# Attention of a hybrid diffusion layer: scores and values in three passes of high and low parts

## Chip, core and metric

One core of a Trainium2 chip. The metric is the device time of one execution of the whole layer, in microseconds; three executions of the kernel before took 1878.99 to 1881.01, median 1880.91.

## What is computed

One layer of a diffusion backbone, all in float32: 512 latent tokens and 256 context tokens of width 2048. A gated DeltaNet branch and a softmax attention branch read one joint input projection; both are gated, projected back, merged and projected out. The change touches the attention alone: 8 query heads, 2 key/value heads, head size 128, 512 queries that see 768 keys (256 of the context, 512 latent).

```python
def block_attention(q, k, v):            # Q_BLOCK = 128
    ...
    scale = hd ** -0.5
    def one_block(qi):
        s = jnp.einsum('bqkgd,bskd->bkgqs', qi, k).astype(jnp.float32) * scale
        p = jax.nn.softmax(s, axis=-1).astype(v.dtype)
        return jnp.einsum('bkgqs,bskd->bqkgd', p, v)
    ...
q_lat = axial_rope(head_rms(bq, B_HEADS, q_norm_w), cos, sin)
k_lat = axial_rope(head_rms(bk, B_KV, k_norm_w), cos, sin)
keys = jnp.concatenate([k_ctx, k_lat], axis=1)
vals = jnp.concatenate([v_ctx, v_lat], axis=1)
b_lat = block_attention(q_lat, keys, vals) * jax.nn.silu(bz)
```

## The kernel before, in words

Every engine has its own hand-written program; semaphores order them, and within an engine the order is that of the code. All the large projections are made in three passes: a float32 operand is split into a high part, rounded to the fp32r type by a copy on ACT (`hi_part`, L759, for weights), and a low part, the rest, by a subtraction on VectorE (`lo_part`, L1091). `three` (L1607) multiplies high by high, high by low and low by high into one PSUM bank. The weights come in pieces of 512 KB, read by SyncE into two buffers in turn; a buffer is read again once both parts of its piece are made. Attention alone has plain float32 matmuls, which TensorE does in two recorded passes each.

The attention stretch comes after the projection of the queries (`bq`) and before the merge. In it the projection of the DeltaNet branch (`pa`, 16 pieces) is interleaved with attention: 32 blocks, block i being head h = i // 4 and 128 queries qt = i % 4. Ahead of the blocks the queries of heads 0 to 3 and the keys are transposed (L1874, L1885) into banks 0 to 7, and ACT copies them out (`q_columns`, `khT`).

- **TensorE**, block i: scores of block i + 1 (L1902, L1903; banks 0 and 1 or 2 and 3), at the first block of a head the values of the head before (L1915, bank 6), half a projection piece (bank 7), in the third block of heads 3 to 6 the transposes of the next head's queries (bank 6), and six transposes of block i's probabilities (L1935, banks 4 and 5).
- **ACT**, iteration i: the exponential of block i + 1 (`att_exp`, L1038), in even iterations the high part of the next weights, the copy of the transposed probabilities of block i (L1052, `probsT`), then queries' squares (blocks 0 to 3), a square root (block 4), the queries' copy, and the high part of the gated output (`b_hi`).
- **VectorE**, iteration i: row sum's reciprocal and scaling of block i (L1512), the maximum of block i + 1 (`att_max`, L1489), in each second block of a head `b_parts` (b_tmp, L1497, and b_lo, L1499, which waits for b_hi), then in odd iterations the gating of a finished piece (`pa_gated`, L1506, frees bank 7) and in even ones the low part of the next weights. In iterations 6, 7, 10 and 11 one tile each of heads 4 to 7 is scaled and rotated (`q_tile(1, t)`, L1356 and L1337 to L1342).
- **GpSimd** issues the transfers of the gates and of gated pieces.

After block 31 come the first piece of the merge (`N_MERGE0`), the values of head 7, and the rest of the merge; at the same time the gates and x are read again.

## Time and profile before

| | us |
|---|---|
| median of three executions | 1880.91 |
| the profiled execution | 1878.7 |
| its span, first to last instruction | 1876.5 |
| TensorE busy | 1800.9 (96%) |
| VectorE busy | 909.9 (48%) |
| ScalarE (ACT) busy | 661.4 (35%) |
| GpSimd busy | 278.1 (15%) |

The profile gives each instruction's start and length. A matmul's length covers its way through the array and overlaps the next one's, so the cost of a matmul in a stream is the distance of two starts. The idle time shown before an instruction names what released it. The mean granted clock of TensorE is 0.99 of full speed.

### The profile page before, as it was taken

The page shows a single profiled execution, that of the slowest core. Times are in us where ns is not written, and L with a number is a line of the kernel's source. Part 1 is how long each engine was busy: PE and PEld are TensorE (multiplying, and loading weights), DVE is VectorE, ACT ScalarE, POOL GpSimd, SP SyncE. Part 2 cuts the span into 40 slices and gives each one's busy share as a digit, 9 for nine tenths or more (in the row PEclk, how much of TensorE's full clock was granted, in tenths as well). Part 3 has the DMA queues.
Part 4 walks back from the last instruction along what each step waited for, and adds up shares of the span by engine and source line. Part 5 has one row for each costly group of instructions (what it writes and reads, how often), then busy time and mean ns, then how long its engine had stood idle before and what let it go on. Part 6 is the DMA issues. An engine that isn't in the chain of part 4 may idle for free.

```text
span 1876.5 us, 25273 instructions
## 1 busy us (share of the span) xinstructions
PE 1800.9 (96%) x10174; PEld 1441.6 (77%) x10174; DVE 909.9 (48%) x1595; ACT 661.4 (35%) x1211; POOL 278.1 (15%) x421
## 2 busy tenths in 40 slices
PE   5799999999999999999999999999998889999999
PEld 2367888888787888878888887877875566788887
DVE  1244443556524577545556554754455544453334
ACT  4323332223234555444343435422354333232211
POOL 0000000000003366377000003211000100210000
PEclk9899999999999999999999999999999999999999
DMA  8793112223224666645444337777432222652332
GB/s 303 245 326 124 57 57 57 63 73 90 70 60 153 197 181 182 203 149 146 136 126 131 115 94 226 231 213 211 140 113 87 87 87 73 257 191 96 118 124 101
DMA packets 198685, 267.12 MB, mean 142 GB/s; under 512 B 37073, under 2 KB 135626, under 8 KB 197162
## 3 DMA queue, kind: packets, MB, share of 16 engines
q1 hardware_dynamic: 175241, 192.74, 34.1%
q0 software_dynamic: 15552, 58.62, 9.4%
q10 hardware_dynamic: 7776, 14.16, 2.0%
q8 instruction: 80, 1.31, 0.3%
q14 instruction: 36, 0.29, 0.0%
HBM read 221.96 MB, written 43.52 MB: 141 GB/s over the span
## 4 chain that ended last, share of the span: by engine, by line
PE 85%; ACT 4%; DVE 4%; DMA 4%; issue 2%; POOL 0%; SPq 0%; ACTq 0%; DVEq 0%; POOLq 0%
PE psum L1610 23%; PE psum L1611 22%; PE psum L1612 22%; PE psum L1915 2%; PE psum L1758 2%; PE psum L1707 1%; PE psum L1709 1%; PE psum L1935 1%; PE psum L1902 1%; PE psum L1603 1%; PE psum L1715 1%; DVE w_lo L1091 1%; ACT w_hi L759 1%; PE psum L1711 1%; PE psum L1713 1%
## 5 line engine op out<-in xcount | busy, mean ns | idle before, releaser
L1091 DVE TENSOR_TENSOR w_lo<-w_raw,w_hi 128x1024 fp32r<-128x1024 f32 x232 | 290.7, 1253 | 625.9 <-ACT w_hi L759 625.6
L759 ACT ACTIVATE w_hi<-w_raw 128x1024 fp32r<-128x1024 f32 x232 | 245.6, 1058 | 864.5 <-PE psum L1612 774.6
L1610 PE MATMUL psum<-h_hi,w_hi 128*128 128x512 f32 x1152 | 470.8, 409 | 8.7 <-DVE w_lo L1091 6.4
L1611 PE MATMUL psum<-h_lo,w_hi 128*128 128x512 f32 x1152 | 452.6, 393 | 0.0
L1612 PE MATMUL psum<-h_hi,w_lo 128*128 128x512 f32 x1152 | 452.1, 392 | 0.0
L1610 PEld LDWEIGHTS psum<-h_hi,w_hi 128*128 128x128 f32 x1152 | 218.2, 189 | 68.2 <-issue 19.4
L1612 PEld LDWEIGHTS psum<-h_hi,w_lo 128*128 128x128 f32 x1152 | 217.5, 189 | 48.1
L1611 PEld LDWEIGHTS psum<-h_lo,w_hi 128*128 128x128 f32 x1152 | 218.5, 190 | 36.2
L1161 DVE SCALAR_TENSOR_TENSOR conv_acc<-conv_in,convw,conv_acc 128x772 f32<-128x772 f32 x96 | 98.2, 1023 | 3.4
L1610 PE MATMUL psum<-w_hi,m_hi 128*128 128x512 f32 x256 | 99.6, 389 | 0.0
L1611 PE MATMUL psum<-w_lo,m_hi 128*128 128x512 f32 x256 | 99.6, 389 | 0.0
L1612 PE MATMUL psum<-w_hi,m_lo 128*128 128x512 f32 x256 | 99.6, 389 | 0.0
L593 POOL TENSOR_TENSOR decay_rhs_hi<-consts,g_hi 128x512 fp32r<-128x512 f32 x24 | 27.0, 1126 | 469.4 <-PE psum L1612 407.7
L1610 PE MATMUL psum<-w_hi,h_hi 128*128 128x512 f32 x192 | 75.5, 393 | 2.5 <-ACT gate_stage L1017 1.3
L1612 PE MATMUL psum<-w_hi,h_lo 128*128 128x512 f32 x192 | 74.8, 389 | 0.0
L1611 PE MATMUL psum<-w_lo,h_hi 128*128 128x512 f32 x192 | 74.7, 389 | 0.0
L1611 PE MATMUL psum<-hc_lo,w_hi 128*128 128x256 f32 x256 | 72.3, 283 | 0.0
L1612 PE MATMUL psum<-hc_hi,w_lo 128*128 128x256 f32 x256 | 72.3, 282 | 0.0
L1610 PE MATMUL psum<-hc_hi,w_hi 128*128 128x256 f32 x256 | 71.9, 281 | 0.0
L1610 PE MATMUL psum<-a_hi,w_hi 128*128 128x512 f32 x128 | 57.2, 447 | 10.2 <-DVE pa_stage L1506 10.2
L1758 PE MATMUL psum<-w_raw_mod,silu_c 128*2 128x512 f32 x256 | 52.1, 668 | 7.0 <-DMA w_raw_mod<-w_mod_dram 6.1
L624 POOL TENSOR_TENSOR inv_blocks<-inv_blocks,inv_outer 128x30 f32<-128x30 f32 (+14 forms) x90 | 55.2, 613 | 7.1
(306 smaller groups left out, 2750.3 us busy)
## 6 DMA issues: line engine op xcount, KB each, us to landing
w_raw<-w_in_dram SPq DMA_DIRECT2D x168, 512.0 KB, 3.9
w_raw_mod<-w_mod_dram SPq DMA_DIRECT2D x64, 512.0 KB, 5.7
w_raw_modg<-w_mod_dram POOLq DMA_DIRECT2D x32, 512.0 KB, 4.5
w_raw<-w_out_dram SPq DMA_DIRECT2D x32, 512.0 KB, 3.6
gate_scratch<-gate_stage ACTq DMA_DIRECT2D x48, 256.0 KB, 4.4
w_raw<-w_proj_a_dram SPq DMA_DIRECT2D x16, 512.0 KB, 4.1
w_raw<-w_proj_b_dram SPq DMA_DIRECT2D x16, 512.0 KB, 3.4
gates<-gate_scratch POOLq DMA_DIRECT2D x32, 256.0 KB, 4.0
```

The costliest lines, as they stand in the source:

```text
L593: ins = pool.tensor_tensor(part_t[d][:], mask, g_t[:, col:col + 4].bitcast(f32).unsqueeze(2).to_broadcast([P, 4, P]), ALU.mult)
L624: pool.tensor_tensor(below, below, outer, ALU.add).then_inc(S("block_steps"), 1)
L759: act.activation(part(whi[i % 2], p), part(place, p), ACT.Copy).then_inc(S("w_hi"), 1)
L1091: dve.tensor_tensor(part(wlo[i % 2], p), part(raw_of(n)[0], p), part(whi[i % 2], p).bitcast(f32), ALU.subtract).then_inc(S("w_lo"), 1)
L1161: ins = dve.scalar_tensor_tensor(out=a[:], in0=r[:, tap:tap + 772], scalar=w, in1=a[:], op0=ALU.mult, op1=ALU.add)
L1603: ins = pe.matmul(bank(7, 1, off + t * 8 + it["head"]), a[:, a0:a0 + P], ones[:, 0:1], start=True, stop=True)
L1610: pe.matmul(out_ap, lh, rh, start=first, stop=False, skip_group_check=shared)
L1611: pe.matmul(out_ap, lh, rl, start=False, stop=False, skip_group_check=shared)
L1612: return pe.matmul(out_ap, ll, rh, start=False, stop=last, skip_group_check=shared)
L1707: ins = pe.matmul(ps[:, u, :], kT_of(h, tile), SS[:, d, h, :], start=True, stop=True)
L1758: ins = pe.matmul(bank(b0)[c0:c0 + 2], sc2[:, k, :], part3(place, p)[:, kk, :], start=k < 4, stop=k >= KT - 4)
L1915: ins = pe.matmul(bank(6), kvr[:, t, 256 + kv * P:256 + (kv + 1) * P], PTt[:, t, :], start=(t == 0), stop=(t == NT - 1))
```

## The change

Queries, keys, values and transposed probabilities are each split into a high fp32r part, which ACT's copy out of PSUM now writes, and a low part, which VectorE subtracts; scores and values then go through `three`. The places of the new tiles are buffers that are idle at the time. The copies on ACT that were plain before are now high parts (same instructions); the values get a copy of their own. VectorE gets the subtractions of queries, keys, values and, once a block, probabilities (`pt_lo_part`), and whoever waited for the copy now waits for the low part.

Besides, the order changes. ACT makes the weights' high part and copies the queries ahead of the exponential. TensorE transposes the queries right after the scores, ahead of the projection, and makes the values after the projection half instead of before it. VectorE's `b_parts` is divided: b_tmp stays, b_lo follows the gating of the piece or the weights' low part. The rotation of heads 4 to 7 runs in eight halves, in iterations 5 to 12. Four semaphores for zeroed buffers become one that counts them in the same order.

```diff
     pa_gate = [at(f"pa_gates{i}", [P, 512], A_H + 53248 + 2048 * i) for i in range(2)]
     pa_out = [at(f"pa_stage{i}", [P, 512], A_H + 57344 + 2048 * i) for i in range(2)]
     sqj = at("square_out", [P, P], A_T + 12288)
-    qhT = at("att_qT", [P, HEADS, SEQ], A_H)
-    khT = at("att_kT", [P, KV, TOK], A_H + 16384)
-    PTt = at("probsT", [P, NT, SEQ], A_H + 34816)
+    q_hi = at("att_q_hi", [P, HEADS, SEQ], A_H, f32r)
+    q_lo = at("att_q_lo", [P, HEADS, SEQ], G_V + 16384, f32r)
+    k_hi = at("att_k_hi", [P, KV, TOK], A_H + 16384, f32r)
+    k_lo = [at(f"att_k_lo{kv}", [P, TOK], (A_H + 30720, A_T + 8192)[kv], f32r) for kv in range(KV)]
+    v_hl = at("att_v", [P, NT, 512], A_C + 16384, f32r)
+    pt_hi = at("probsT_hi", [P, NT, SEQ], A_H + 34816, f32r)
+    pt_lo_a = at("probsT_lo_a", [P, 4, 1024], A_C, f32r)
+    pt_lo_b = at("probsT_lo_b", [P, 2, SEQ], G_V + 12288, f32r)
+    pt_lo_c = at("probsT_lo_c", [P, NT, SEQ], A_H, f32r)
     atmp = [at(f"a_tmp{i}", [P, 512], A_C + 2048 * i) for i in range(2)]
     probs = [at(f"probs{i}", [P, TOK], A_H + 47104 + 3072 * i) for i in range(2)]
     cs = at("cos_sin", [P, LT, 128], G_V)
...
             if g["kind"] == "pa":
                 if g["m"] == 0:
                     eng.wait_ge(S("a_lo"), HEADS)
-                    eng.wait_ge(S("kt_evac"), KV)
+                    eng.wait_ge(S("att_lo"), 6)
                 else:
                     eng.wait_ge(S("pa_mul"), g["m"])
             if g["kind"] == "merge":
...
 
             def q_columns(h, b):
                 act.wait_ge(S("qt_ready"), h + 1)
-                act.activation(qhT[:, h, :], bank(b), ACT.Copy).then_inc(S("qt_evac"), 1)
+                act.activation(q_hi[:, h, :], bank(b), ACT.Copy).then_inc(S("qt_evac"), 1)
 
             for kv in range(KV):
                 q_columns(2 * kv, 2 * kv)
                 q_columns(2 * kv + 1, 2 * kv + 1)
                 act.wait_ge(S("kt_ready"), kv + 1)
-                act.activation(khT[:, kv, :], PS[:, (4 + 2 * kv) * 512:(4 + 2 * kv) * 512 + TOK], ACT.Copy).then_inc(
+                act.activation(k_hi[:, kv, :], PS[:, (4 + 2 * kv) * 512:(4 + 2 * kv) * 512 + TOK], ACT.Copy).then_inc(
                     S("kt_evac"), 1)
 
             def att_exp(i):
...
 
             att_exp(0)
             for i in range(32):
+                h, qt = divmod(i, 4)
+                if i % 2 == 0:
+                    hi_part(N_PA0 + i // 2 + 1)
+                if qt == 2 and 3 <= h < 7:
+                    q_columns(h + 1, 6)
                 if i < 31:
                     att_exp(i + 1)
-                if i % 2 == 0:
-                    hi_part(N_PA0 + i // 2 + 1)
-                h, qt = divmod(i, 4)
                 if qt == 0 and h >= 1:
                     act.wait_ge(S("pv_done"), h)
                 act.wait_ge(S("pt_ready"), i + 1)
-                act.activation(PTt[:, :, qt * P:(qt + 1) * P],
+                act.activation(pt_hi[:, :, qt * P:(qt + 1) * P],
                                PS[:, 2048:2048 + TOK].rearrange("p (t n) -> p t n", t=NT), ACT.Copy).then_inc(
                     S("pt_evac"), 1)
                 if i < 4:
                     q_squares(1, i)
                 if i == 4:
                     qk_std(3, 16, 32)
-                if qt == 2 and 3 <= h < 7:
-                    q_columns(h + 1, 6)
+                if i == 1:
+                    act.activation(v_hl[:, :, 0:256], kvr[:, :, 256:512], ACT.Copy).then_inc(S("kt_evac"), 1)
                 if qt == 1 and h >= 1:
                     act.wait_ge(S("b_tmp"), h)
                     act.activation(b_hi[:, h - 1, :], btmp[:], ACT.Copy).then_inc(S("b_hi"), 1)
...
                             ln(dve.tensor_tensor(tab[:, :, 128 * hf + 64 * sn:128 * hf + 64 * sn + 64],
                                                  cs[:, :, 64 * sn:64 * sn + 64], wv, ALU.mult))
 
-            def rope(rows_t, tab_t, nh):
+            def rope_products(rows_t, tab_t, nh):
 
                 x1, x2 = rows_t[:, :, 0:64], rows_t[:, :, 64:128]
                 tv = lambda k: tab_t[:, 64 * k:64 * k + 64].unsqueeze(1).to_broadcast([P, nh, 64])
                 ln(dve.tensor_tensor(rt[0][:, 0:nh, :], x1, tv(0), ALU.mult))
                 ln(dve.tensor_tensor(rt[1][:, 0:nh, :], x2, tv(3), ALU.mult))
+
+            def rope_sums(rows_t, tab_t, nh):
+
+                x1, x2 = rows_t[:, :, 0:64], rows_t[:, :, 64:128]
+                tv = lambda k: tab_t[:, 64 * k:64 * k + 64].unsqueeze(1).to_broadcast([P, nh, 64])
                 ln(dve.tensor_tensor(rt[2][:, 0:nh, :], x1, tv(1), ALU.mult))
                 ln(dve.tensor_tensor(rt[3][:, 0:nh, :], x2, tv(2), ALU.mult))
                 ln(dve.tensor_tensor(x1, rt[0][:, 0:nh, :], rt[1][:, 0:nh, :], ALU.subtract))
                 return dve.tensor_tensor(x2, rt[2][:, 0:nh, :], rt[3][:, 0:nh, :], ALU.add)
 
+            def rope(rows_t, tab_t, nh):
+                rope_products(rows_t, tab_t, nh)
+                return rope_sums(rows_t, tab_t, nh)
+
             def qk_var(count, a0, a1):
                 dve.wait_ge(S("qk_ssq"), count)
                 dve.tensor_scalar(ssq_a[:, a0:a1], ssq_a[:, a0:a1], 1.0 / P, EPS, ALU.mult, ALU.add).then_inc(
...
                 dve.wait_ge(S("qk_std"), step)
                 ln(dve.reciprocal(ssq_a[:, a0:a1], ssq_a[:, a0:a1]))
 
-            def q_tile(j, t):
+            def q_tile(j, t, parts=(0, 1)):
                 rv = bqr[:, t, 512 * j:512 * j + 512].rearrange("p (h n) -> p h n", h=4)
-                sv = ssq_a[:, 16 * j + 4 * t:16 * j + 4 * t + 4].unsqueeze(2).to_broadcast([P, 4, P])
-                ln(dve.tensor_tensor(rv, rv, sv, ALU.mult))
-                rope(rv, qtab[:, t, :], 4).then_inc(S("q_rot"), 1)
+                if 0 in parts:
+                    sv = ssq_a[:, 16 * j + 4 * t:16 * j + 4 * t + 4].unsqueeze(2).to_broadcast([P, 4, P])
+                    ln(dve.tensor_tensor(rv, rv, sv, ALU.mult))
+                    rope_products(rv, qtab[:, t, :], 4)
+                if 1 not in parts:
+                    return
+                rope_sums(rv, qtab[:, t, :], 4).then_inc(S("q_rot"), 1)
 
                 dve.wait_ge(S("q_rot"), 4 * j + t + 1)
 
...
                 dve.tensor_scalar(nmax[:, i:i + 1], nmax[:, i:i + 1], -float(HD ** -0.5), None, ALU.mult).then_inc(
                     S("negmax"), 1)
 
-            def b_parts(h):
+            def b_gated(h):
                 dve.wait_ge(S("pv_done"), h + 1)
                 k = HEADS + h
                 dve.wait_ge(S(f"z_in{k % 2}"), 16 * (k // 2 + 1))
                 dve.tensor_tensor(btmp[:], bank(6), zst[k % 2][:], ALU.mult).then_inc(S("b_tmp"), 1)
+
+            def b_lo_part(h):
                 dve.wait_ge(S("b_hi"), h + 1)
                 dve.tensor_tensor(b_lo[:, h, :], btmp[:], b_hi[:, h, :].bitcast(f32), ALU.subtract).then_inc(S("b_lo"), 1)
 
...
                     dve.wait_ge(S(f"pa_spill{m % 2}"), 16 * (m // 2))
                 dve.tensor_tensor(pa_out[m % 2][:], bank(7), pa_gate[m % 2][:], ALU.mult).then_inc(S("pa_mul"), 1)
 
+            def q_lo_part(h, b):
+                dve.wait_ge(S("qt_evac"), h + 1)
+                dve.tensor_tensor(q_lo[:, h, :], bank(b), q_hi[:, h, :].bitcast(f32), ALU.subtract).then_inc(S("att_lo"), 1)
+
+            def pt_lo_part(i):
+                h, qt = divmod(i, 4)
+                own = slice(qt * P, qt * P + P)
+                dve.wait_ge(S("pt_evac"), i + 1)
+                src = PS[:, 2048:2048 + TOK].rearrange("p (t n) -> p t n", t=NT)
+                if h >= 6:
+                    dve.tensor_tensor(pt_lo_c[:, :, own], src, pt_hi[:, :, own].bitcast(f32), ALU.subtract).then_inc(S("pt_lo"), 1)
+                    return
+                dve.tensor_tensor(pt_lo_a[:, :, own], src[:, 0:4], pt_hi[:, 0:4, own].bitcast(f32), ALU.subtract)
+                dve.tensor_tensor(pt_lo_b[:, :, own], src[:, 4:6], pt_hi[:, 4:6, own].bitcast(f32), ALU.subtract).then_inc(
+                    S("pt_lo"), 1)
+
+            for kv in range(KV):
+                q_lo_part(2 * kv, 2 * kv)
+                q_lo_part(2 * kv + 1, 2 * kv + 1)
+                if kv:
+                    for i in range(2):
+                        dve.wait_ge(S(f"gate_spill{i}"), 16 * len(GATES))
+                dve.wait_ge(S("kt_evac"), kv + 1)
+                dve.tensor_tensor(k_lo[kv][:], PS[:, (4 + 2 * kv) * 512:(4 + 2 * kv) * 512 + TOK],
+                                  k_hi[:, kv, :].bitcast(f32), ALU.subtract).then_inc(S("att_lo"), 1)
+
             att_max(0)
             for i in range(32):
                 dve.wait_ge(S("exp_done"), i + 1)
                 ln(dve.reciprocal(rsum[:, i:i + 1], rsum[:, i:i + 1]))
                 dve.tensor_scalar(probs[i % 2][:], probs[i % 2][:], rsum[:, i:i + 1], None, ALU.mult).then_inc(
                     S("p_norm"), 1)
+                if i:
+                    pt_lo_part(i - 1)
                 if i < 31:
                     att_max(i + 1)
+                if i % 4 == 2 and 3 <= i // 4 < 7:
+                    q_lo_part(i // 4 + 1, 6)
                 if i % 4 == 1 and i >= 5:
-                    b_parts(i // 4 - 1)
+                    b_gated(i // 4 - 1)
                 if i % 2:
                     pa_gated(i // 2)
                 else:
                     lo_part(N_PA0 + i // 2 + 1)
-
+                if i % 4 == 1 and i >= 5:
+                    b_lo_part(i // 4 - 1)
+
+                if i == 2:
+                    dve.wait_ge(S("kt_evac"), 3)
+                    dve.tensor_tensor(v_hl[:, :, 256:512], kvr[:, :, 256:512], v_hl[:, :, 0:256].bitcast(f32),
+                                      ALU.subtract).then_inc(S("att_lo"), 1)
                 if i == 4:
                     qk_var(44, 16, 32)
                 if i == 5:
                     qk_rstd(3, 16, 32)
-                if i in (6, 7, 10, 11):
-                    q_tile(1, (6, 7, 10, 11).index(i))
+                if 5 <= i < 13:
+                    q_tile(1, (i - 5) // 2, ((i - 5) % 2,))
+            pt_lo_part(31)
             lo_part(N_MERGE0 + 1)
-            b_parts(HEADS - 1)
+            b_gated(HEADS - 1)
+            b_lo_part(HEADS - 1)
             for n in range(N_MERGE0, NP):
                 if n > N_MERGE0:
                     lo_part(n + 1)
...
                 h, qt = divmod(i, 4)
                 if i < 2:
 
-                    pe.wait_ge(S("qt_evac"), 2 * i + 2)
-                    pe.wait_ge(S("kt_evac"), i + 1)
+                    pe.wait_ge(S("att_lo"), 3 + 2 * i)
                 else:
                     pe.wait_ge(S("exp_done"), i - 1)
                 if h >= 4 and qt == 0:
-                    pe.wait_ge(S("qt_evac"), h + 1)
+                    pe.wait_ge(S("att_lo"), h + 4)
                 b = 2 * (i % 2)
-                q = qhT[:, h, qt * P:(qt + 1) * P]
+                q = tuple(part[:, h, qt * P:(qt + 1) * P] for part in (q_hi, q_lo))
                 kv = h // (HEADS // KV)
-                pe.matmul(bank(b), q, khT[:, kv, 0:512], start=True, stop=True)
-                pe.matmul(bank(b + 1, 256), q, khT[:, kv, 512:TOK], start=True, stop=True).then_inc(S("sc_ready"), 1)
+                three(bank(b), q, (k_hi[:, kv, 0:512], k_lo[kv][:, 0:512]), True, True)
+                three(bank(b + 1, 256), q, (k_hi[:, kv, 512:TOK], k_lo[kv][:, 512:TOK]), True, True).then_inc(S("sc_ready"), 1)
 
             def values(h):
 
-                pe.wait_ge(S("pt_evac"), 4 * h + 4)
+                pe.wait_ge(S("pt_lo"), 4 * h + 4)
                 if h >= 1:
                     pe.wait_ge(S("b_tmp"), h)
+                if h == 0:
+                    pe.wait_ge(S("att_lo"), 7)
                 if 3 <= h < 7:
 
-                    pe.wait_ge(S("qt_evac"), h + 2)
+                    pe.wait_ge(S("att_lo"), h + 5)
                 kv = h // (HEADS // KV)
                 for t in range(NT):
-                    ins = pe.matmul(bank(6), kvr[:, t, 256 + kv * P:256 + (kv + 1) * P], PTt[:, t, :],
-                                    start=(t == 0), stop=(t == NT - 1))
+                    lo = pt_lo_c[:, t, :] if h >= 6 else pt_lo_a[:, t, 0:SEQ] if t < 4 else pt_lo_b[:, t - 4, :]
+                    v = tuple(v_hl[:, t, half + kv * P:half + (kv + 1) * P] for half in (0, 256))
+                    ins = three(bank(6), v, (pt_hi[:, t, :], lo), t == 0, t == NT - 1)
                 ins.then_inc(S("pv_done"), 1)
 
             scores(0)
...
                 if i < 31:
                     scores(i + 1)
                 h, qt = divmod(i, 4)
+                if qt == 2 and 3 <= h < 7:
+
+                    pe.wait_ge(S("b_tmp"), h)
+                    q_transposes(h + 1, 6)
+                piece(N_PA0 + i // 2, (i % 2,))
                 if qt == 0 and h >= 1:
                     values(h - 1)
-                piece(N_PA0 + i // 2, (i % 2,))
-                if qt == 2 and 3 <= h < 7:
-
-                    pe.wait_ge(S("b_tmp"), h)
-                    q_transposes(h + 1, 6)
                 pe.wait_ge(S("p_norm"), i + 1)
                 if i:
-                    pe.wait_ge(S("pt_evac"), i)
+                    pe.wait_ge(S("pt_lo"), i)
                 for t in range(NT):
                     ins = pe.transpose(PS[:, 2048 + t * P:2048 + (t + 1) * P], probs[i % 2][:, t * P:(t + 1) * P], ident)
                 ins.then_inc(S("pt_ready"), 1)
...
                 if n > N_MERGE0:
                     piece(n)
                 if n == N_MERGE0 + 1:
-                    pe.wait_ge(S("pt_evac"), 32)
+                    pe.wait_ge(S("pt_lo"), 32)
                     pe.wait_ge(S("b_tmp"), HEADS)
                     pe.wait_ge(S("pa_mul"), 16)
                     pe.wait_ge(S("gsum_in"), 16)
```

## Rows read from the trace of the kernel before

**Rows 1.** The page's first part: busy us, share of the span, instructions.

```profile
PE 1800.9 (96%) x10174; PEld 1441.6 (77%) x10174; DVE 909.9 (48%) x1595; ACT 661.4 (35%) x1211; POOL 278.1 (15%) x421
```

**Rows 2.** Stretches: window, length, busy per engine (instructions), TensorE's clock, DMA share, GB/s.

```profile
1387.70:1601.20 213.50, 192.70 (x805) 132.76 (x805) 108.74 (x204) 88.75 (x161) 19.18 (x35) 1.00 0.28 86
...
1613.00:1629.00 16.00, 16.00 (x65) 11.87 (x64) 7.02 (x9) 4.54 (x6) 2.15 (x4) 1.00 1.01 395
```

**Rows 3.** Timeline of TensorE, block 9: start, us, instruction [idle before].

```profile
1446.20 0.82 PE L1935 MATMUL psum<-consts,probs 128*128 128x128 f32 x6
1446.85 1.02 PE L1902 MATMUL psum<-att_kT,att_qT 128*128 128x512 f32 x2
...
1448.38 0.40 PE L1611 MATMUL psum<-a_lo,w_hi 128*128 128x512 f32 x1
...
1450.92 0.82 PE L1935 MATMUL psum<-consts,probs 128*128 128x128 f32 x6
```

**Rows 4.** The same in the convolution stage: six passes of 256 columns lie between.

```profile
301.60 0.28 PE L1610 MATMUL psum<-hc_hi,w_hi 128*128 128x256 f32 x1
...
302.31 0.40 PE L1610 MATMUL psum<-h_hi,w_hi 128*128 128x512 f32 x1
```

**Rows 5.** The same, one head's values and the projection pass behind.

```profile
1438.18 5.42 PE L1915 MATMUL psum<-probsT,kv_rows 128*128 128x512 f32 x12 [0.61 <-ACT probsT L1052]
...
1443.66 0.39 PE L1611 MATMUL psum<-a_lo,w_hi 128*128 128x512 f32 x1
```

**Rows 6.** Transposes of probabilities: all (ns, first and last start), then blocks 4, 12, 28.

```profile
L1935 PE MATMUL psum<-consts,probs x192: 270/272/331, 1393.6 to 1601.1; 128*128 128x128 f32 x192
...
1417.61 0.82 PE L1935 MATMUL psum<-consts,probs 128*128 128x128 f32 x6
...
1474.52 0.82 PE L1935 MATMUL psum<-consts,probs 128*128 128x128 f32 x6
...
1586.02 0.82 PE L1935 MATMUL psum<-consts,probs 128*128 128x128 f32 x6
```

**Rows 7.** Timeline of three engines, blocks 13 to 15, the gaps of a head.

```profile
1481.45 0.69 DVE L1499 TENSOR_TENSOR b_lo<-b_tmp,b_hi 128x512 fp32r<-128x512 f32 x1 [3.02 <-ACT b_hi L1063]
1482.06 0.68 DVE L1506 TENSOR_TENSOR pa_stage<-psum,pa_gates 128x512 f32<-128x512 f32 x1
...
1482.80 0.50 PE L1610 MATMUL psum<-a_hi,w_hi 128*128 128x512 f32 x1 [1.45 <-DVE pa_stage L1506]
...
1488.41 1.10 PE L1902 MATMUL psum<-att_kT,att_qT 128*128 128x512 f32 x2 [1.48 <-ACT att_qT L1025]
```

**Rows 8.** Groups, 1380 to 1600: busy us, mean ns | idle before, releasers.

```profile
L1489 DVE TENSOR_REDUCE neg_max<-psum 128x1 f32<-128x768 f32 x32 | 30.6, 955 | 44.8 <-PE psum L1903 44.8
L1038 ACT ACTIVATE probs<-psum,neg_max 128x768 f32<-128x768 f32 x32 | 28.9, 902 | 73.8 <-DVE neg_max L1490 72.1 <-ACT square_out L888 1.5
...
L1052 ACT ACTIVATE probsT<-psum 128x768 f32<-128x768 f32 x31 | 25.1, 810 | 48.2 <-PE psum L1935 48.1
L1611 PEld LDWEIGHTS psum<-a_lo,w_hi 128*128 128x128 f32 x128 | 24.1, 188 | 6.4 <-issue 1.7
...
L1091 DVE TENSOR_TENSOR w_lo<-w_raw,w_hi 128x1024 fp32r<-128x1024 f32 x17 | 20.8, 1226 | 33.3 <-ACT w_hi L759 33.3
L1512 DVE TENSOR_SCALAR probs<-probs,row_sum 128x768 f32<-128x768 f32 x32 | 19.9, 621 | 1.1
...
L888 ACT ACTIVATE square_out<-bq_rows 128x128 f32<-128x128 f32 x16 | 5.0, 309 | 0.4
...
L1337 DVE TENSOR_TENSOR rope<-bq_rows,q_tab 128x256 f32<-128x256 f32 x4 | 1.7, 425 | 0.1
```

**Rows 9.** Timeline of the start: first copies, first scores, first projection pass.

```profile
1385.81 1.12 ACT L1025 ACTIVATE att_qT<-psum 128x512 f32<-128x512 f32 x2
...
1387.78 1.10 PE L1902 MATMUL psum<-att_kT,att_qT 128*128 128x512 f32 x2 [0.87 <-ACT att_kT L1031]
...
1390.64 0.59 PE L1610 MATMUL psum<-a_hi,w_hi 128*128 128x512 f32 x1
```

24 lines of the change are left out of this document (12 added, 12 removed).

## Prediction

> **What bounds the kernel now.** I read the page's busy times first: TensorE is busy 96% of the span [rows 1]. So only two things shorten this kernel: fewer TensorE cycles, or fewer of the few gaps it has. Next the busy times by stretch: the attention stretch, from the first scores to the last transposes, takes 213.5 us with TensorE busy 192.7, at a granted clock of 1.00 [rows 2]; some 21 of the kernel's 76 idle microseconds lie there, more than anywhere behind the opening. Then the timeline of one block of 128 queries, which gives the real cadence of the matmuls (the mean duration of one overlaps its neighbour's and is too long): transposes 1446.20 to 1446.85, so 0.65 us; then the scores and twelve passes of the projection, until the next transposes at 1450.92 [rows 3]. Eleven of these passes lie between 1448.38 and 1450.92: 0.231 us each for 512 columns. Twelve take 2.77, so of the block's 4.72 us the scores have 4.72 - 0.65 - 2.77 = 1.30 us.
>
> **TensorE's own work.** Passes of fp32r tiles with 256 columns come six in 302.31 - 301.60, 0.12 us each [rows 4]. New scores: 3 x 0.231 + 3 x 0.12 = 1.05, saving 0.25 in each of 32 blocks: 8.0 us. Values before: from 1438.18 to the second projection pass at 1443.66, less that one pass, 5.25 us a head [rows 5]. New: 18 passes x 0.231 = 4.16, saving 1.09 in each of 8 heads: 8.7 us. Together 16.7 us, all on TensorE, which is the bound. A plain block becomes 1.05 + 2.77 + 0.65 = 4.47 us, one with values 8.63, one with the four query transposes (heads 4 to 7) 4.47 + 4 x 0.11 = 4.91.
>
> **The gaps it has.** The transposes of blocks 12 and 28 begin at 1474.52 and 1586.02 [rows 6], so a later head takes 27.9 us. In each of these heads TensorE waits 1.45 us for pa_stage, since VectorE had stood 3.02 us before b_lo for ACT's b_hi, with pa_stage queued behind it; and 1.48 us for att_qT, the queries' copy queued behind w_hi and probsT on ACT [rows 7]. The four blocks and one set of values cost 4 x 4.72 + 5.25 = 24.1 us, 24.6 with query transposes; so 3.3 us a head are gaps. From the first transposes (1393.6) to those of block 31 (the last of six starts at 1601.1 [rows 6], the first 0.55 earlier) are 207.0 us; its work is 31 x 4.72 + 7 x 5.25 + 4 x 0.44 - 1.3 (no scores in the last) = 183.5; gaps 23.5 in all.
>
> **What VectorE gets.** A subtraction reading PSUM, 512 wide, takes 0.68 and releases VectorE after 0.61; 1024 from SBUF 1.23 [rows 7, 8]; the nearest row for 256 is a rope product, 0.43, and the next instruction follows 0.36 later. pt_lo (512 + 256) is then 0.97 us; q_lo 0.61; k_lo 0.88; v_lo (1536) by the line through 512 and 1024 1.77, and its ACT copy 1.5. No row shows such a subtraction with this strided output. Bounds for pt_lo: 0.88 (one pass of 768 with its overlap taken off; a reduction of 768 takes 0.96 [rows 8]) to 1.4 (two full ones of 512); I take 0.97, nearest in size and source. All together VectorE gains 32 x 0.97 + 8 x 0.61 + 2 x 0.88 + 1.77, some 40 us of work. New waits: transposes of block i wait for pt_lo of i-1, which itself waits for pt_hi (0.81); scores wait for q_lo and k_lo; values wait for pt_lo and v_lo.
>
> **A steady head, walked through.** Times from the start t of the transposes of a values block (block 4h). Durations are those of rows 8, with about 0.05 us from one engine to the next, as in rows 7. pt_hi starts at t + 0.87, pt_lo runs 1.72 to 2.69, though the next scores are ready at 1.90. The reduction and scaling hold VectorE 1.10 (to 3.79), exp runs 3.87 to 4.90 with its accumulator read. b_gated goes in the gap, to 4.40; pa_gated waits for the projection, 4.67 to 5.28: bank 7 is wanted at t + 4.47 + 0.65 + 1.05 = 6.17, so the 1.45 us stall goes. b_hi now stands behind pt_hi and ends at 6.66, b_lo at 7.31; only VectorE waits. Then normalising (0.73) to 8.04 and pt_lo to 9.0, 9.13 for TensorE, which comes to the second transposes after t + 4.47 at 8.94 (9.38 with query transposes): a stall of 0.19 or none. The w_lo of this block starts at once, since ACT made w_hi before the exponential, and q_lo goes in the same way. The third block ends 0.5 before TensorE needs it, and in the fourth the values' 4.16 us let VectorE catch up. The queries' copy, now before the projection, is 2.8 us of work ahead of the next need: that 1.48 goes too. A head takes 3 x 4.47 + 8.63 + 0.44, or + 0.19, 22.5 us instead of 27.9. From block 12 to 28: 90.0 instead of 111.5, gain 21.5. Blocks 28 to 31: 14.5 become 3 x 4.47 + 0.19 - 1.05 = 12.55, gain 1.9.
>
> **Heads with rotation (blocks 5 to 12).** The halves put a scaling and two products (1.64) or two products and two sums (1.84) [rows 8] into every block instead of 3.5 in every other. Per four blocks VectorE has 4 x 2.8 for normalising, pt_lo and reduction, 2 x 1.15 for w_lo, 4 x 0.61, and 7.0 of rotation: 22.9, plus some 2 of waits on ACT. That is above TensorE's 22.0: here VectorE paces. Walked block by block the transposes of blocks 6, 7, 8, 10 and 11 come late by 2.1, 1.3, 0.6, 1.9 and 1.3 us. Blocks 4 to 12 then take 51.8 instead of 56.9 (1417.61 to 1474.52 [rows 6]). Gain 5.1.
>
> **The first four blocks.** The values' copy (1.5) follows ACT's four squares of block 1 (0.31 each and a read of the accumulator behind it [rows 8]); behind it wait w_hi and the third exp; VectorE then does w_lo and v_lo (1.77). The transposes of block 3 come 2.1 us late, and block 4 is reached after 24.1 us, as before. Gain 0, where the passes alone would give 2.1.
>
> **The start.** Scores 0 began at 1387.78, after two queries' copies and a key's [rows 9]. VectorE's three subtractions each follow theirs and end 0.9 later; six in all hold VectorE until 1390.65 (first copy done 1386.43, the copies' pace until 1387.7, then three of 0.61 to 0.88). The first projection pass wants k_lo 1 and scores 1: 1391.0 instead of 1390.64; transposes 0 start 0.2 later. Loss 0.2.
>
> **The end.** The last values save 1.1, but a DMA-full stretch follows, share 1.01 from 1613 [rows 2], in which the weights of the next merge piece are awaited. Between nothing and 1.1: I take 0.5. The renamed zeroing semaphore counts the same memsets in the same order: nothing. No DMA is added, and the reloads come as their buffers come free, 9 us a piece against some 4 to land.
>
> **Sum.** -0.2 + 0 + 5.1 + 21.5 + 1.9 + 0.5 = 28.8. The profiled execution took 1878.7 (span 1876.5 and 2.2 around it), the median is 1880.9; I take the gain from each: 1849.9 for a profiled run, **1852** for the median. Of the 28.8, some 16 are cheaper passes and 13 gaps closed.
>
> **Where a page differs.** Loads and passes overlap in these rows: a load is 188 ns [rows 8], longer than the 0.12 between 256-column passes. The Trainium skill (TensorE: Matmul & The Clock Gate, Part 3, The mechanism) says that weight loads overlap running matmuls only with different row groups; here all rows are used by every pass. By that rule added loads would stand on the path; the trace disagrees. The same page allows, in its Part 2, a background buffer, which agrees.
>
> **Rivals.** (a) The passes get cheaper and the gaps stay: VectorE's new work fills what the reordering freed, so that each head keeps its 3.3 us. Gain 16.7 less the 0.6 at the end and 0.2 at the start: 1865. For it: VectorE holds the transposes now. Against: the walk leaves slack in three blocks of four. 15%. (b) The gaps go almost fully, since halves of the rotation slip into slack I counted as used: 23 + 16 = 39, 1842. 5%. (c) Weight loads don't hide for the added passes: 336 loads (6 x 32 + 18 x 8) instead of 224, 112 x 0.19 = 21 us: 1873. Against it the rows above. 2%. (d) Slower: VectorE becomes the bound everywhere, because a subtraction from PSUM with this output pattern is far dearer. A steady head's VectorE work is 16.6 and its waits 1.4; it ties with the old 27.9 when pt_lo costs 3.4 us, and at 4.4 each head takes 31.7, or 30 us more than before: 1911. 3%, as no shape in the trace is above 1.3 ns a column. (e) The new tiles aren't taken as fp32r, and three full passes run: 2 x (32 x 1.30 + 8 x 5.25) = 167 us more, 2048. The tiles are declared as those of the projection, 1%.
>
> **From these to the numbers.** The forecast has 74%, with its own range 1845 to 1860 (pt_lo between 0.88 and 1.4 moves the rotation blocks and a little of each head: -1 to +8; the end and the start by 1). Taking in most of (a) gives 1845 to 1865. What counts as no change here is within 0.2%, 3.8 us, about what a measurement can tell. Faster 0.95, same 0.01, slower 0.04.
>
> **What would show it.** In the changed profile: six score passes in 1.05 us and eighteen of values in 4.16; plain blocks every 4.47 us; the stalls on pa_stage and att_qT gone; transposes waiting for pt_lo only in the rotation blocks; heads after block 12 every 22.5 us. Heads of 25 us or more, with transposes waiting for pt_lo throughout, would make (a) right and this wrong; a b_lo or w_lo on the critical chain would show that the walk's order on VectorE is off.

## The result, and the profile after

| | before | after |
|---|---|---|
| median of four executions, us | 1879.95 | 1854.88 |
| lowest to highest | 1876.03 to 1881.01 | 1851.49 to 1855.64 |
| the profiled execution | 1878.7 | 1851.49 |
| its span | 1876.5 | 1849.2 |

After to before is 0.9868, with a 95% interval of 0.9856 to 0.988: the change takes 25.1 us off, where 28.8 were forecast. The page of after answers to [rows 1]:

```profile
PE 1781.2 (96%) x10286; PEld 1456.5 (79%) x10286; DVE 947.0 (51%) x1662; ACT 661.9 (36%) x1212; POOL 277.5 (15%) x421
```

TensorE has 112 matmuls more and 19.7 us less to do; VectorE has 37.1 us more. The stretch of [rows 2], 213.50 us long before, is now the first line below. The second line runs from the first transposes of probabilities to those of block 31, and is the yardstick for all that follows (window, length, then busy us and instructions of TensorE, its weight loads, VectorE, ACT and GpSimd, granted clock, DMA share, GB/s):

```profile
1386.30:1573.50 187.20, 175.60 (x904) 145.24 (x905) 142.40 (x268) 88.78 (x162) 19.08 (x35) 1.00 0.32 98
1391.95:1573.50 181.55, 170.51 (x881) 141.06 (x881) 137.88 (x260) 84.36 (x155) 19.08 (x35) 1.00 0.32 96
```

The same yardstick in the kernel before:

```profile
1393.60:1600.60 207.00, 186.43 (x780) 128.41 (x778) 105.42 (x197) 84.81 (x155) 19.18 (x35) 1.00 0.27 83
```

I call the start of block i's six transposes T(i) and the start of the first query transposes Q. What lies ahead of Q is not touched by the change, and Q itself came anywhere from 1379.5 to 1386.0 in the profiled runs below; so kernels are compared by stretches between these starts, and whole times only by their medians. A block is named by the transposes that end it: block i lasts from T(i - 1) to T(i). TensorE's timeline of after, which answers to [rows 6], shows where transposes still wait. The lines are T(0), T(3), T(4), T(6), T(12) and T(31):

```profile
1391.95 0.82 PE L1998 MATMUL psum<-consts,probs 128*128 128x128 f32 x6
...
1407.28 0.85 PE L1998 MATMUL psum<-consts,probs 128*128 128x128 f32 x6 [1.79 <-DVE probsT_lo_b L1544]
1415.84 0.81 PE L1998 MATMUL psum<-consts,probs 128*128 128x128 f32 x6
...
1427.08 0.84 PE L1998 MATMUL psum<-consts,probs 128*128 128x128 f32 x6 [2.15 <-DVE probsT_lo_b L1544]
...
1467.55 0.82 PE L1998 MATMUL psum<-consts,probs 128*128 128x128 f32 x6
...
1573.50 0.85 PE L1998 MATMUL psum<-consts,probs 128*128 128x128 f32 x6 [0.22 <-DVE probsT_lo_c L1541]
```

| us | before | after | gain | forecast |
|---|---|---|---|---|
| ahead of Q | 1383.69 | 1381.87 | 1.8 | none of the change's |
| Q to T(0) | 9.91 | 10.08 | -0.2 | -0.2 |
| T(0) to T(4) | 24.01 | 23.89 | 0.1 | 0 |
| T(4) to T(12) | 56.91 | 51.71 | 5.2 | 5.1 |
| T(12) to T(28) | 111.50 | 93.02 | 18.5 | 21.5 |
| T(28) to T(31) | 14.58 | 12.93 | 1.65 | 1.9 |
| behind T(31) | 275.90 | 275.70 | 0.2 | 0.5 |
| T(0) to T(31) | 207.00 | 181.55 | 25.5 | 28.5 |

In the profiled pair 1.8 us of the 27.2 between the two executions lie ahead of Q and are none of the change's. The row that came out differently is the steady heads, those behind block 12. A head of them has blocks of 4.48, 4.90, 5.36 and 8.56 us from one T to the next; the forecast had 4.47, 4.91, 4.47 and 8.63. The third is block 15 and its like, whose scores are the first of the next head. All three engines there, after:

```profile
1475.06 0.59 ACT L1031 ACTIVATE att_q_hi<-psum 128x512 fp32r<-128x512 f32 x1
...
1476.51 0.95 DVE L1510 TENSOR_REDUCE neg_max<-psum 128x1 f32<-128x768 f32 x1
...
1476.93 0.82 PE L1998 MATMUL psum<-consts,probs 128*128 128x128 f32 x6
...
1477.57 0.68 DVE L1533 TENSOR_TENSOR att_q_lo<-psum,att_q_hi 128x512 fp32r<-128x512 f32 x1
...
1478.39 0.47 PE L1671 MATMUL psum<-att_k_hi,att_q_hi 128*128 128x512 f32 x1 [0.65 <-DVE att_q_lo L1533]
...
1479.16 0.28 PE L1671 MATMUL psum<-att_k_hi,att_q_hi 128*128 128x256 f32 x1
...
1486.77 0.39 PE L1671 MATMUL psum<-probsT_hi,att_v 128*128 128x512 f32 x1
...
1490.85 0.82 PE L1998 MATMUL psum<-consts,probs 128*128 128x128 f32 x6
```

The queries' high part is made by 1475.65, but the low part stands on VectorE behind the maximum of block 15, which holds it to 1477.57, and the scores of block 16, ready to start at 1477.5 when the transposes end, wait for it. The two lines at the end, start of the values and start of the next transposes, give the 18 passes of the values 4.08 us. And the groups of after that answer to [rows 8] (busy us, mean ns of one | idle before, releaser):

```profile
L1543 DVE TENSOR_TENSOR probsT_lo_a<-psum,probsT_hi 128x512 fp32r<-128x512 f32 x24 | 16.5, 686 | 14.8 <-ACT probsT_hi L1060 14.8
L1544 DVE TENSOR_TENSOR probsT_lo_b<-psum,probsT_hi 128x256 fp32r<-128x256 f32 x24 | 10.0, 415 | 0.0
L1541 DVE TENSOR_TENSOR probsT_lo_c<-psum,probsT_hi 128x768 fp32r<-128x768 f32 x8 | 7.6, 955 | 10.6 <-ACT probsT_hi L1060 10.6
L1580 DVE TENSOR_TENSOR att_v<-kv_rows,att_v 128x1536 fp32r<-128x1536 f32 x1 | 1.8, 1752 | 0.0
```

The waits of the attention stretch, after (who waits for whom: us in total, times, longest):

```profile
DVE b_lo L1522 <- ACT b_hi L1071: 9.4, 7, 1.4
PE psum L1998 <- DVE probsT_lo_b L1544: 7.7, 5, 2.2
PE psum L1671 <- DVE att_q_lo L1533: 2.5, 4, 0.6
```

Two of the three gaps of [rows 7] are gone: no matmul waits for pa_stage, none for the queries' copy. The third, b_lo behind b_hi, is there still, 1.4 us at most instead of 3.02. In the steady heads TensorE waits for nothing that is queued behind it. In block 6 it does: behind this b_lo VectorE has the first rotation and pt_lo, for which T(6) waits 2.15 us.

```profile
1422.65 0.69 DVE L1522 TENSOR_TENSOR b_lo<-b_tmp,b_hi 128x512 fp32r<-128x512 f32 x1 [1.44 <-ACT b_hi L1071]
```

### The profile page after: what moved, and what is told of

It reads as the page before. It is cut to its first block, busy times and chain, and to the rows that moved or that the text cites. A ratio compares the mean times of both kernels' runs of the same rounds, so it can differ in the third digit from the quotient of the medians.

```text
span 1849.2 us, 25568 instructions
## 1 busy us (share of the span) xinstructions
PE 1781.2 (96%) x10286; PEld 1456.5 (79%) x10286; DVE 947.0 (51%) x1662; ACT 661.9 (36%) x1212; POOL 277.5 (15%) x421
## 4 chain that ended last, share of the span: by engine, by line
PE 82%; DVE 7%; DMA 4%; ACT 4%; issue 2%; POOL 1%; SPq 0%; ACTq 0%; DVEq 0%; POOLq 0%
PE psum L1671 23%; PE psum L1673 22%; PE psum L1672 22%; PE psum L1819 2%; DMA w_raw_mod<-w_mod_dram 1%; PE psum L1768 1%; PE psum L1770 1%; DVE w_lo L1099 1%; PE psum L1664 1%; PE psum L1776 1%; ACT w_hi L765 1%; PE psum L1772 1%; PE psum L1774 1%; DMA w_raw<-w_proj_b_dram 1%; PE psum L1998 1%
## 5 line engine op out<-in xcount | busy, mean ns | idle before, releaser
L1672 PEld LDWEIGHTS psum<-w_lo,m_hi 128*128 128x128 f32 x256 | 48.0, 188 | 10.1
L1673 PEld LDWEIGHTS psum<-w_hi,m_lo 128*128 128x128 f32 x256 | 48.0, 188 | 10.0
```

The lines of the kernel that those rows point to most:

```text
L1672: pe.matmul(out_ap, lh, rl, start=False, stop=False, skip_group_check=shared)
L1673: return pe.matmul(out_ap, ll, rh, start=False, stop=last, skip_group_check=shared)
```

## The experiments

Two theories stood at the start. **O**: the order alone closes the gaps, and most of the gain is the order's. **P**: cheaper passes are what pays, and the order only makes room for VectorE's new work. The prediction booked both, 16 us to the passes and 13 to the gaps. After that came the stall on q_lo, and what VectorE's work costs. e6, e7, e9 and e10 were executed once each, so their stretches are read and not their whole times. Stretches of all kernels, in us:

| kernel | Q to T(0) | T(0) to T(4) | T(4) to T(12) | T(12) to T(28) | T(28) to T(31) | T(0) to T(31) |
|---|---|---|---|---|---|---|
| before | 9.91 | 24.01 | 56.91 | 111.50 | 14.58 | 207.00 |
| after | 10.08 | 23.89 | 51.71 | 93.02 | 12.93 | 181.55 |
| e1 order only | 9.90 | 24.03 | 49.72 | 97.89 | 12.83 | 184.47 |
| e2 passes only | 10.08 | 30.70 | 71.17 | 116.21 | 15.60 | 233.68 |
| e3 q_lo first | 11.66 | 23.48 | 51.65 | 89.50 | 12.92 | 177.55 |
| e4 values' parts later | 10.12 | 21.97 | 51.69 | 93.01 | 12.93 | 179.60 |
| e5 scores only | 10.08 | 23.01 | 48.95 | 93.84 | 12.35 | 178.15 |
| e6 ACT's old order | 11.65 | 25.29 | 57.94 | 113.15 | 15.00 | 211.38 |
| e7 pt_lo twice | 10.07 | 26.54 | 58.87 | 101.72 | 15.25 | 202.38 |
| e8 all moved | 11.68 | 21.91 | 44.87 | 89.49 | 12.92 | 169.19 |
| e9 TensorE's old order | 10.09 | 27.72 | 58.72 | 98.42 | 12.93 | 197.79 |
| e10 VectorE's old order | 10.10 | 23.88 | 59.77 | 95.72 | 14.35 | 193.72 |

### The order alone: e1_order_only

The kernel before, with float32 matmuls and no low parts, in the order of after:

```
+                if qt == 2 and 3 <= h < 7:
+                    q_columns(h + 1, 6)
                 if i < 31:
                     att_exp(i + 1)
...
-                if qt == 0 and h >= 1:
-                    values(h - 1)
                 piece(N_PA0 + i // 2, (i % 2,))
+                if qt == 0 and h >= 1:
+                    values(h - 1)
```

with the weights' high part likewise ahead of `att_exp`, `b_parts` divided, and the rotation in halves, as in after.

> The kernel before with the changed order alone (w_hi and queries' copy ahead of the exponential, query transposes ahead of the projection, values behind it, b_lo behind the gating, rotation in halves), float32 matmuls kept. Theory O (the order closes the gaps, whatever the matmuls cost): TensorE's work from the first to the last transposes stays 183.5 us and of the 23.5 us of gaps at most 3 stay, so 184 to 187 us instead of 207.0, in all some 1859 (1857 to 1861), ratio 0.988 to 0.990. Rival A (passes and order add up as the result's 25 us less 16.7 for cheaper passes): 8 to 9 us from the order, 1871.

Median 1851.95 against 1875.22, ratio 0.9873 (0.9859 to 0.9888). The stretch took 184.47 us. Its work, by the prediction's cadences, is 183.5; of 23.5 us of gaps 1.0 is left. Its window:

```profile
1391.80:1576.00 184.20, 182.99 (x778) 128.54 (x777) 104.95 (x197) 83.76 (x154) 18.84 (x35) 1.00 0.31 95
```

Theory O holds: the order alone gives 22.5 of the 25.5 us that the stretch gained, without one cheaper pass, and the two medians' ratios are not told apart.

### The passes alone: e2_passes_only

After's parts and passes, with all four orders (ACT's, TensorE's, the two of VectorE's) put back:

```
-                piece(N_PA0 + i // 2, (i % 2,))
                 if qt == 0 and h >= 1:
                     values(h - 1)
+                piece(N_PA0 + i // 2, (i % 2,))
...
-                if 5 <= i < 13:
-                    q_tile(1, (i - 5) // 2, ((i - 5) % 2,))
+                if i in (6, 7, 10, 11):
+                    q_tile(1, (6, 7, 10, 11).index(i))
```

> The changed kernel with its subtractions and three passes but the order of before. Theory O: the work falls by 16.7 us, yet pt_lo and q_lo lengthen the two chains on which a head waited (pa_stage behind b_hi, scores behind the queries' copy), so that each head still takes 26.5 to 28 us and the whole 1870 to 1880. Rival A (they add up): 1863 to 1865, heads of 25.8 us (27.9 less 4 x 0.25 and 1.09).

Median 1900.73 against 1875.22, ratio 1.0142 (1.0115 to 1.0168): 25 us slower than before, and worse than either theory had it. The window and the waits:

```profile
1390.30:1624.00 233.70, 186.24 (x881) 151.69 (x881) 138.34 (x260) 85.31 (x156) 19.28 (x35) 0.93 0.24 74
```

```profile
PE psum L1670 <- DVE probsT_lo_b L1544: 12.7, 6, 4.8
PE psum L1670 <- DVE pa_stage L1529: 12.0, 7, 1.8
PE psum L1997 <- DVE probsT_lo_b L1544: 10.7, 4, 3.7
PE psum L1670 <- DVE att_q_lo L1533: 10.2, 4, 2.6
```

The low parts of the probabilities and of the queries are now waits of TensorE: the values (L1670 behind probsT_lo_b) wait for the last block's, the transposes for the same, the scores for q_lo, which waits for ACT's copy behind the exponential. The old wait for pa_stage is there too. Cheaper passes in the old order cost more than they bring. That also explains why the two parts do not add: with the order, the passes give 184.47 - 181.55 = 2.9 us; without it they cost 233.68 - 207.00 = 26.7. The clock has a share in it, some 10 us (mean of the stretch 0.93; see the last section).

### The three orders one by one: e6_act_order, e9_pe_order, e10_vector_order

Each is after with one engine's order put back. e6: ACT makes the exponential first, then the weights' high part, the probabilities' copy, and the queries' copy behind these.

```
-                if qt == 2 and 3 <= h < 7:
-                    q_columns(h + 1, 6)
                 if i < 31:
                     att_exp(i + 1)
...
+                if qt == 2 and 3 <= h < 7:
+                    q_columns(h + 1, 6)
```

> The changed kernel with ACT's old order: w_hi behind the exponential, the queries' copy behind the probabilities' copy. Theory: the three orders (ACT, TensorE, VectorE) carry the passes together; this one alone undone makes w_lo wait for w_hi in every second block and the next head's scores for q_hi: heads of 26 us, stretch 200 to 208. Rival (only the VectorE order counts): within 2 us of 181.6.

1888.23 us, stretch 211.38, 29.8 more than after. ACT, VectorE and TensorE in it, at the scores of a new head:

```profile
1492.27 0.80 ACT L1058 ACTIVATE probsT_hi<-psum 128x768 fp32r<-128x768 f32 x1
1492.96 0.59 ACT L1031 ACTIVATE att_q_hi<-psum 128x512 fp32r<-128x512 f32 x1
1493.59 0.69 DVE L1533 TENSOR_TENSOR att_q_lo<-psum,att_q_hi 128x512 fp32r<-128x512 f32 x1 [3.19 <-ACT att_q_hi L1031]
1494.42 0.77 PE L1671 MATMUL psum<-att_k_hi,att_q_hi 128*128 128x512 f32 x1 [3.93 <-DVE att_q_lo L1533]
```

The queries' copy stands behind the probabilities' on ACT, the low part stands 3.19 us and with it all of VectorE's queue, and TensorE stands 3.93. It came out dearer than expected; the clock fell here too (mean of the stretch 0.94), which is some 6 of the 29.8 us.

e9: the values ahead of the projection half, the diff as in e2's first lines.

> The changed kernel with TensorE's old order: values ahead of the projection half, query transposes behind it. Theory (each of the three orders is needed once the parts are on VectorE): the values, reached 1.7 us after the last transposes began, wait for pt_lo, ready at 3.4 to 4.5, 2 to 3 us a head; with the query transposes late, the exponential behind the queries' copy and then q_lo are late too. Heads of 26 us, stretch 200 to 210 instead of 181.6, more if the clock falls in a wait. Rival (TensorE's order is of little weight, the ACT order did it all): within 3 us of 181.6.

1869.20 us, stretch 197.79, 16.2 more than after and below the 200 to 210 expected. Some 3 us of it are passes at half clock behind two of the waits. Values blocks of the first heads take 12.38, 11.85 and 13.44 us instead of 8.56 and 9.14. The waits of TensorE and ACT:

```profile
PE psum L1671 <- DVE probsT_lo_b L1544: 10.7, 6, 3.0
ACT att_q_hi L1031 <- PE psum L1935: 7.9, 4, 2.0
```

In after, twelve projection passes (2.8 us) stand between the scores and the values and cover pt_hi and pt_lo; here the values follow the scores.

e10: VectorE's b_lo ahead of the gating of the piece, and the rotation in whole tiles.

```
                     b_gated(i // 4 - 1)
+                    b_lo_part(i // 4 - 1)
```

> The changed kernel with VectorE's old order: b_lo ahead of the gating of the piece, whole tiles rotated in blocks 6, 7, 10 and 11. Theory: bank 7 is gated 7.9 us after the transposes began and wanted at 6.2, 1.9 us a head of waiting for pa_stage, and the next transposes 0.6 late; stretch 196 to 202. Rival (b_hi is ready by then, as ACT is nearly idle): within 3 us of 181.6.

1863.80 us, stretch 193.72, 12.2 more. The steady blocks are 4.48, 6.43, 4.48 and 8.53: now the second block of a head is late, and q_lo, wanted after it, is there in time. The waits, then one such place:

```profile
PE psum L1670 <- DVE pa_stage L1529: 10.3, 7, 1.8
DVE b_lo L1522 <- ACT b_hi L1071: 15.9, 7, 2.4
```

```profile
1555.31 0.50 PE L1670 MATMUL psum<-a_hi,w_hi 128*128 128x512 f32 x1 [1.26 <-DVE pa_stage L1529]
```

In the steady heads this is the gap of [rows 7] come back. But 8.1 of the 12.2 us lie between T(4) and T(12), where the whole tiles of rotation are: blocks 8 and 12 take 12.55 and 12.58 us instead of 9.14, as the values wait 2.1 us for pt_lo behind a whole tile and then run at half clock. So e10 undoes two orders, and the places say what each cost. None of the three engines' orders can be left out: undone singly they cost 29.8, 16.2 and 12.2 us, in sum 58.2, undone together 52.1, the falls of the clock included.

### The stall of 0.65 us: e3_qlo_first

After, with the queries' low part ahead of the next maximum on VectorE:

```
-                if i < 31:
-                    att_max(i + 1)
                 if i % 4 == 2 and 3 <= i // 4 < 7:
                     q_lo_part(i // 4 + 1, 6)
+                if i < 31:
+                    att_max(i + 1)
```

> The changed kernel with q_lo ahead of the next block's maximum on VectorE. Theory Q: in blocks 15, 19, 23 and 27 the first scores of a head wait for q_lo (0.65 us idle, block of 5.36 us instead of 4.48), because it stands behind the maximum; put ahead, these blocks take 4.5 us and the stretch is 3.5 us shorter: 1851.4. Rival (the delayed maximum and exponential make the next transposes late by as much): these blocks fall but their neighbours grow, no difference, 1854.9.

Steady heads took 89.50 us instead of 93.02: 3.5 less, blocks 15, 19, 23 and 27 fell from 5.36 to 4.46, and the whole stretch from 181.55 to 177.55. The place of this one instruction made the stall that the prediction had not seen; this is shown. The median, 1849.16 (ratio 0.986, 0.984 to 0.9879), is not told apart from after's by the intervals of the two ratios; in its profiled run 1.6 of the 4.0 us were lost again ahead of T(0) (11.66 instead of 10.08, last section).

### The values' parts a block later: e4_v_later

```
-                if i == 1:
+                if i == 2:
                     act.activation(v_hl[:, :, 0:256], kvr[:, :, 256:512], ACT.Copy).then_inc(S("kt_evac"), 1)
...
-                if i == 2:
+                if i == 3:
                     dve.wait_ge(S("kt_evac"), 3)
```

> The changed kernel with the values' copy and subtraction one block later (copy after block 2 on ACT, subtraction in block 3 on VectorE). Theory V: the 1.8 us stall before the transposes of block 3 comes from this copy ahead of w_hi and the exponential and from v_lo in VectorE's block 2; one block later the values of head 0, 4 us long, cover it, the stall goes and block 4 is reached 1.8 to 2.0 us sooner: 1853. Rival: it only moves, as v_lo then holds up block 4: 1854.9.

T(0) to T(4) 21.97 instead of 23.89; block 3 went from 6.43 to 4.46, and the other stretches stayed. So the forecast's "2.1 us late" of T(3) was real, 1.96, and the values' parts made it. Median 1852.35, ratio 0.9871 (0.9848 to 0.9894): 2 us are under what medians tell here.

### Three passes for the scores alone: e5_scores_only

e3 with the transposed probabilities as a plain float32 copy and the values as before; no pt_lo, no parts of the values:

```
-                    ins = three(bank(6), v, (pt_hi[:, t, :], lo), t == 0, t == NT - 1)
+                    ins = pe.matmul(bank(6), kvr[:, t, 256 + kv * P:256 + (kv + 1) * P], PTt[:, t, :],
+                                    start=(t == 0), stop=(t == NT - 1))
```

> The changed order with three-pass scores (q_lo, k_lo; q_lo ahead of the maximum) but plain float32 values, so no pt_lo, no v_lo: VectorE is spared 33 us. Theory V2 (the passes' gain is paid back by VectorE's subtraction of the probabilities, so the cheap half is the scores): order alone took 184.5 us from first to last transposes; scores save 0.25 x 31 = 7.8, and gaps stay near those of the order alone, so 177 to 178 us, 4 us less than the whole change with both in three passes (181.6). Rival (the gaps of the changed kernel come from q_lo, the copies' order and the values' copy, not from pt_lo): no better than the changed kernel, 181 or more.

Stretch 178.15, at the edge of what was expected; median 1849.12 against 1876.86, ratio 0.9851 (0.9835 to 0.9866). It is 3.4 us under after's, but q_lo's place alone gives 4.0 of that. Compared with e3, which has q_lo in the same place, the three-pass values gain 93.84 - 89.50 = 4.3 us in the steady heads and lose 51.65 - 48.95 = 2.7 in the blocks with rotation and 1.0 in the other two stretches: 0.6 us net for 7.6 us less work of TensorE (7 heads by 1.09). Their price is pt_lo, 0.97 us in each block, 31 us of VectorE, and the values' own parts. This holds for this order: e5's matmuls alone make 175.7 us (183.5 less 31 x 0.25), and e8 below, with the values in three passes, takes 169.19.

### VectorE's load doubled: e7_ptlo_twice

```
+                ln(dve.tensor_tensor(pt_lo_b[:, :, own], src[:, 4:6], pt_hi[:, 4:6, own].bitcast(f32), ALU.subtract))
+                dve.tensor_tensor(pt_lo_a[:, :, own], src[:, 0:4], pt_hi[:, 0:4, own].bitcast(f32), ALU.subtract)
```

Each subtraction of pt_lo is issued twice; the second writes what the first did.

> The changed kernel with every subtraction pt_lo made twice (same result), 1.0 us more on VectorE per block. If VectorE has 2 to 3 us of slack in a later head (my walk), heads after block 12 go from 23.3 to 25 to 26 us and the rotation blocks grow by the whole 1.0 each: stretch from 181.6 to some 202. If VectorE is the bound already everywhere, every block grows by 1.0: 213. If it has slack throughout, 185.

1871.20 us, stretch 202.38, 20.8 us over after, for some 31 us of added work: 7.2 of it in the eight blocks with rotation, 8.7 in the sixteen steady ones, where a head goes from 23.3 to 25.4. So 7.2 of 7.8 added us show where the rotation runs, and 8.7 of 15.5 even in the steady blocks, where VectorE was thought to have room in three blocks of four. In both stretches the clock fell once (mean of the whole stretch 0.98); block 23, 7.10 us where its like take 5.55, has the second of these falls, so part of the 8.7 is the clock's.

### What was left, taken away: e8_all_moved

e3 and e4 together, and the rotation of heads 4 to 7 moved out of the crowded blocks: a head at a time instead of a tile of queries, in the blocks whose values give VectorE room, with a copy of the table that the next pieces don't overwrite.

```
+                if i == 4:
+                    ln(dve.tensor_copy(qtab2[:], qtab[:]))
+                if i in (8, 12, 16, 20):
+                    q_head((i - 8) // 4)
...
-                pe.wait_ge(S("q_rot"), LT if h < 4 else 2 * LT)
+                pe.wait_ge(S("q_rot"), LT if h < 4 else LT + h - 3)
```

> The changed kernel with q_lo ahead of the maximum, the values' copy one block later, and the rotation of heads 4 to 7 made a head at a time (four tiles of one head, same instructions) in blocks 8, 12, 16 and 20, where the values hold TensorE 4.2 us, from a copy of its table. Theory: rotation costs nothing there; blocks 4 to 12 take 44.5 us instead of 51.7, the whole stretch 169 to 171 instead of 181.6, TensorE's work being 168.4; median 10 to 12 us below the changed kernel. Rival (VectorE has no such slack in the values' blocks): these blocks grow beyond 8.6 us and the stretch stays above 174.

Its window:

```profile
1391.20:1560.40 169.20, 168.41 (x882) 141.35 (x880) 136.60 (x259) 83.65 (x155) 19.10 (x35) 1.00 0.34 103
```

The stretch took 169.19 us, against 168.4 of work by the prediction's cadences: all gaps are gone but 0.8 us. T(4) to T(12) is 44.87 instead of 51.71, with VectorE doing nearly the same work as in after (136.60 and 137.88): what it lacked was not time in all but time in those blocks. Most of the 0.8 us is block 6, which takes 5.12: the 1.44 us before b_lo are there still. Median **1840.69** (1838.44 to 1844.34) against 1876.86, ratio 0.9814 (0.9794 to 0.9835): it beats both kernels, after by some half a per cent, the intervals of the two ratios not touching.

What the cheaper passes are worth therefore depends on where the new work stands. TensorE's work with float32 matmuls is 183.5 us by the same cadences, so no order of e1's instructions could come near 169.19: some 14 us are the passes' here, against 2.9 between e1 and after. That is an estimate from these cadences, not a run; e1 with e8's rotation was not measured.

## Why the prediction was right, and where it was off

- **The bound** was read rightly: TensorE at 96%, so cycles and gaps. Its work came out as sized. The cadences of the prediction (0.231, 0.12 and 0.65 us) give 183.5 and 168.4 us for the stretch, and e1 and e8, which have nearly no gaps, took 184.47 and 169.19.
- **Each new instruction** was sized rightly: pt_lo 0.97 (records of 686 and 415 ns, which overlap), v_lo 1.77 (1.75), 18 passes 4.16 (4.08). The strided output costs nothing that shows.
- **Start, first four blocks, rotation:** -0.2, 0.1 and 5.2 us against -0.2, 0 and 5.1, with the stalls where the walk had them: T(3) late by 1.96 (2.1 forecast; its wait is 1.79), block 6 at 6.76 us, 2.3 over a plain one (2.1), block 7 at 5.68 (1.2 over; 1.3), block 10 at 6.36 (1.9; 1.9), block 11 at 5.68 (1.2; 1.3). Block 8 was 0.6 late, as forecast. Block 12 was taken as free and was 0.57 late. That 5.2 us agree with 5.1 is luck in part: the prediction's own terms, six blocks of 4.47, two of 8.63 and 7.2 us of stalls, make 51.3 us and a gain of 5.6, where it wrote 51.8 and 5.1; the slip is as large as the stall that it missed. e4 shows the cause of the stall at T(3), the values' parts, and e8 that the rotation's place makes nearly all of the others.
- **The step that failed** is a clause in the walk of a steady head: "q_lo goes in the same way". It was followed to where it is issued, not to what stands ahead of it. On ACT the queries' copy is in time, as the prediction said; but the wait has moved one step on. VectorE comes to q_lo only after scaling, pt_lo and the maximum, and the scores start at 1478.39 after 0.65 of idle time; the block takes 0.88 more than a plain one. Four blocks by 0.88 are 3.5 us; the term 21.5 for the steady heads came out as 18.5. e3 removes them and has 22.4 us a head, the forecast's 22.5.
- **Block 31** was 0.4 us over the forecast's, 0.22 of it the wait for probsT_lo_c; 1.65 instead of 1.9.
- **The end** gave 0.2 instead of 0.5. The values do save 1.1, but the merge behind them then waits longer for gate_rows. In e1 and e5, whose values are float32, it does not wait for gate_rows at all, and T(31) to the end takes 274.7 and 274.6 us instead of 275.7. So the term was booked to the wrong part of the change: here too the order gains, and the values in three passes lose 1.0. What makes gate_rows late with them stays open. Before and after:

```profile
1632.92 0.50 PE L1610 MATMUL psum<-b_hi,w_hi 128*128 128x512 f32 x1 [1.06 <-DVE gate_rows L1555]
```

```profile
1605.57 0.50 PE L1671 MATMUL psum<-b_hi,w_hi 128*128 128x512 f32 x1 [1.85 <-DVE gate_rows L1616]
```

- **"Some 16 are cheaper passes and 13 gaps closed"** is near as a count of work and of idle time (15.1 us less work in the stretch; 23.5 us of gaps became 13.2) and wrong as a statement of causes. The order alone closes 22.5; the low parts then open 12.2 again, against 15.1 of saved work (183.5 - 168.4). Taken in this sequence, 22.5 of the 25.5 us are the order's and 2.9 the passes'; taken the other way the passes lose 26.7 and the order gains 52.1, so neither is the share of one part alone. A sum over blocks of the finished kernel can't tell this; only the two halves run singly do.
- **Rival (a)**, the gaps stay, was wrong as a whole but is the mechanism that took back most of what the passes save. **(c)**: 112 loads more cost nothing. A load takes 188 ns in after too, three passes of 256 columns start within 0.24 us (1479.16, 1479.29 and 1479.40), and the steady plain blocks of e8 take 4.45 to 4.48 us, the forecast's 4.47, which has nothing added for loads. So the trace goes against the rule of the Trainium skill (TensorE: Matmul & The Clock Gate, Part 3, The mechanism) that the prediction set beside it, loads overlapping matmuls only where the row groups differ. **(d)** and **(e)** did not occur; the reason given against (d), no shape above 1.3 ns a column, was misread, as a rotation product of 256 columns takes 425 ns [rows 8], 1.66 a column. What bears is pt_lo as measured: 686 ns for 512 columns, 1.34 a column.
- **What was missing among the rivals** is a falling clock. The prediction took 1.00 throughout; that held in the stretch for after, e1, e5 and e8. It fell there in e2, e6, e7, e9 and e10, and for a few us in e3 and e4.

## What to carry to other kernels

When matmuls get cheaper by work on another engine, write down for each new result the queue that it stands in, with all that is ahead of it there, up to the matmul that wants it; a wait that is taken off one engine often goes on at the next. Before adding such work, try the order alone; here it gave nearly all of the gain, and the passes alone lost 1.4%. Then look at the load of the helping engine by block, not by stage: nearly the same 137 us of VectorE cost TensorE 13.2 us of gaps in after and 0.8 in e8, by where q_lo, the values' parts and above all the rotation (6.8 us) stood. Only with that placing did the passes pay in full.
